# Head 0's query and key projections moved into the last attention group of a hybrid decoder step

## The chip, the cores and the metric

The kernel runs on one core of a Trainium2 chip. The metric is device time in microseconds (us) of one execution. Before the change the median of 3 runs is 2359.29 us (2358.37 to 2360.00); one more execution was profiled.

## The reference, cut to what matters

One layer, one step, for a prompt of 1024 tokens and 8 single sample tokens (1032 columns together). The part around the change:

```
h = rms_norm(x); proj = h @ w_in     # [dilated attention q/k/v of 3 groups | DeltaNet q/k/v | z | beta | decay | gates]
# branch A: per group (window, dilation) = (128,1), (512,4), (2048,16): 4 heads of 64, softmax with a relative bias,
#           groups merged by their softmax denominators; the sample tokens attend to cached keys and values
# branch B: per head (8 heads of 128): causal conv of width 4 + SiLU on q/k/v, l2norm, gated delta rule in chunks,
#           gated RMSNorm with silu(z)
x = x + rms_norm((sigmoid(gate_a) * (o_a @ w_a) + sigmoid(gate_b) * (o_b @ w_b)) @ w_out)
x = x + rms_norm((silu(h2 @ w_gate) * (h2 @ w_up)) @ w_ffn_out)      # h2 = rms_norm(x)
```

All is float32. A projection is computed in three passes: weights and inputs are split into a high and a low part, and lo*hi, hi*lo and hi*hi are added in one bank.

## The kernel before, in words

The program is written engine by engine: each engine has its instructions in a fixed order, and semaphores join them. A block of the program ends on all engines before the next begins.

**Attention block** (`attention_block`, L490). It normalises the input, then runs the three groups. A group has a key/value projection, a query projection (`q_part`), and 8 tiles of 128 queries (`tile`). While the tiles of a group run, TensorE fills its waits with the key/value projection of the next group (a `Filler`: a list of numbered steps, worked off up to a given number at given places). The last group (`AHEAD`, g = 2) has no next one, so its filler is empty. A tile is: scores on TensorE (L655), scale and bias, maximum and its negative on VectorE (L827, L832, L835), exponentials on ScalarE (L731), transposes on TensorE (L689), copy by ScalarE (L769), products with the values (L699), copy to `os_` by VectorE (L794), and a store of `os_` from SP's queue (L610). `os_` has two buffers: the maximum of tile t waits for the store of tile t - 2. In the last group the scores are issued two tiles ahead.

**Heads block** (`heads_block`, L2260). Head 0 has a stage of its own (the prologues near the end of the block), later heads are projected while the head before is in its recurrence. A head's projection has tiles m = 2, 3, 4, 5 (q, k, v, z), each of three thirds of 344 columns, each third 8 steps of three matmuls (L293 to L295): step numbers run from 49 to 144. On TensorE a third of tile m waits until the same third of tile m - 1 is read out of its bank (`evac`). ScalarE splits the weights' high part (`hi`, L286), reads the thirds out (L2435, L2437) and does the tanh of each convolution (L2448); VectorE splits the low part (`lo`, L289), does the convolution (L2523 to L2531) and the SiLU (L2501). ScalarE's order per tile, which stays as it is:

```python
if m < end:
    yield n + 2 * KT
    read_out(m, 1)
if before in CONVS:
    yield n + 2 * KT + 2
    tanh_of(CONVS.index(before))
if m < end:
    yield n + 3 * KT
    read_out(m, 2)
```

so the tanh of the tile before stands ahead of the last third's read-out. Between these steps stands the sample tokens' attention over cached keys: query rows (`queries`), spread of the queries over partitions on TensorE (L2063, L2064), scores against the cached keys on VectorE (L2132, L2136), softmax, turned probabilities (L2078), and last the products with the cached values (L2096). The constants for the convolutions (L1962 to L1975) and the weights that merge the groups (L2210 to L2229) stand there as well. Which step numbers come before which of these parts is written in `SPREAD_STEP`, `SC_STEP`, `P_STEP` (L2361). After the products VectorE takes the result (L2181) and clears `ub`, and head 0's recurrence begins.

Of the kernel before, what the change touches and what calls it, by code (L numbers as in the profile page):

```python
# [21 lines left out]
NS = 8  # L22
# [56 lines left out]
def build(nc, a, o):  # L79

    ctx = ExitStack()
    with ctx:
        n_names = [0]

        def sb(stack, name, shape, dt=FP):
            return stack.enter_context(nc.sbuf_tensor(name, shape, dt))

# [402 lines left out]
        def attention_block(used):  # L490

            with ExitStack() as s:
                KV, Q = 2 * HA * HD, HA * HD
                kv_hi = sb(s, "a_kv_hi", [P, KT, KV], FR); q_hi = sb(s, "a_q_hi", [P, KT, Q], FR)

                with ExitStack() as place:
                    kv_raw = sb(place, "a_kv_raw", [P, KT, KV]); q_raw = sb(place, "a_q_raw", [P, KT, Q])
                kv_lo = sb(s, "a_kv_lo", [P, KT, KV], FR); q_lo = sb(s, "a_q_lo", [P, KT, Q], FR)
# [48 lines left out]
                def wt(eng, name, g, k):  # L547
                    if E[name].at(g, k) > 0:
                        eng.wait_ge(E[name].sem, E[name].at(g, k))

# [21 lines left out]
                def _(sp):  # L572
# [11 lines left out]
                    for g in range(NG):  # L584
# [33 lines left out]
                def _(pe):  # L618
# [60 lines left out]
                    def tile(g, t, fill):  # L679
# [12 lines left out]
                        if g == AHEAD and t + 2 < NT:  # L692
                            scores(g, t + 2)
# [9 lines left out]
                        inc(last, "pv")  # L703

# [3 lines left out]

                    beta_pe(pe)
# [3 lines left out]
                def _(act):  # L713
# [45 lines left out]
                    def tile(g, t, fill):  # L759
# [11 lines left out]
                        if g == AHEAD and t + 1 < NT:  # L771
                            exps(g, t + 1)
# [15 lines left out]
                def _(v):  # L788
# [29 lines left out]
                    def tile(g, t, fill):  # L818
# [34 lines left out]
                    groups(v, kv_steps, beta_rest, q_part, tile, 1)  # L853

# [1086 lines left out]
        norm_sems = []  # L1941
        attention_block(norm_sems)
# [50 lines left out]
        def sample_attention(s, v_c, k_c, vec, ten, exped):  # L1993
# [18 lines left out]
            k_ld = [sem("sa_k") for _ in range(NG)]; v_ld = sem("sa_v")  # L2012
# [4 lines left out]
            def load(sp, stage):  # L2017
# [4 lines left out]
                if stage == 0:  # L2022
# [4 lines left out]
                    for g in range(NG):  # L2027
                        sp.dma_start(k_c[g][:NKEY[g]], rows(g, 0)).then_inc(k_ld[g], 16)
# [229 lines left out]
        pre = [sb(hs, f"pre{m}", [P, 3 + T]) for m in range(3)]  # L2258

        def heads_block(used):  # L2260
            s = hs
            w_raw = [sb(s, f"w_raw{j}", [P, KT, P]) for j in range(2)]
            w_hi = [sb(s, f"w_hi{j}", [P, KT, P], FR) for j in range(2)]
            w_lo = [sb(s, f"w_lo{j}", [P, KT, P], FR) for j in range(2)]
# [5 lines left out]
            with ExitStack() as place:  # L2270
# [5 lines left out]
                k_c = [sb(place, f"sa_k{j}", [P, NS, HA * HD]) for j in range(NG)]  # L2276
# [4 lines left out]
            k_tok = sb(s, "k_tok", F8); vb = sb(s, "vb", F8); kbe = sb(s, "kbe", F8); kdec = sb(s, "kdec", F8)  # L2281
# [3 lines left out]
            w_t = sb(s, "w_t", F8); q_dec = sb(s, "q_dec", F8)  # L2285
# [19 lines left out]
            wld = [sem("w_loaded") for j in range(2)]  # L2305
            whi = [ev("w_hi", 3, 1) for j in range(2)]
            wlo = [ev("w_lo", 3, 1) for j in range(2)]
            tile_done = [ev("tile_done", 3, 1) for j in range(2)]
            group = [ev("group", 6, 2) for g in range(2)]
            evac = [ev("evac", 6, 2) for g in range(3)]  # L2310
# [9 lines left out]
                      samp_m=1, cn=3, s_sq=1, s_nm=1, s_ln=1, s_r=1, s_v=4, s_k=1, s_vn=1, s_bc=2, s_o2=1, s_rms=1,  # L2320
                      s_oln=2, s_ob=1, s_add=2, s_dec=1)
            E = {k: ev(k, n, -1 if k in ("ob", "ssq", "s_oln", "s_add") else 0) for k, n in D1.items()}
# [34 lines left out]

            def is_last(h):
                return isinstance(h, int) and h == HB
# [863 lines left out]
```

## Time and profile before

| | us |
|---|---|
| median of 3 runs | 2359.29 |
| profiled execution | 2358.57 |
| its span | 2356.8 |
| TensorE busy | 2238.1 (95%) |
| VectorE busy | 1241.2 (53%) |
| ScalarE busy | 729.2 (31%) |

The span goes from the first to the last instruction; 1.8 us of the execution lie outside it. A timeline row gives start, duration, engine, line, output and inputs, and in brackets how long the engine was idle before and what released it. A window row gives for a stretch its length, and the busy time with the number of instructions of TensorE, its weight loads, VectorE, ScalarE and GpSimd, then TensorE's granted clock as a share of 2.4 GHz (so 0.50 is 1.2 GHz), the DMA share and GB/s. A group row ends with busy us, mean ns of one, and the idle time before.

### The profile page before, as it was taken

The numbers are of one execution on the slowest core, as the hardware profiler recorded it, in microseconds if no ns is written. First come the engines' busy times: TensorE is split into PE (matmuls) and PEld (weight loads), VectorE is DVE, ScalarE is ACT, GpSimd is POOL, SyncE is SP. The second block draws the span as 40 slices with busy tenths as digits, with TensorE's granted clock in tenths as the row PEclk, the third lists the DMA queues.
The fourth block names the chain that finished last, engine by engine and source line by source line (L and its number), as shares of the span: only waits on it lengthen the run. The fifth ranks groups of instructions, "written<-read, shape, count | busy, mean of one in ns | idle before, by whom it ended". The sixth has DMA issues, their size and how long they took to land. (4 is left out here: it accounts for less than half of the span.)

```text
span 2356.8 us, 36214 instructions
## 1 busy us (share of the span) xinstructions
PE 2238.1 (95%) x14552; PEld 2085.2 (88%) x14552; DVE 1241.2 (53%) x2379; ACT 729.2 (31%) x1646; POOL 65.0 (3%) x76
## 2 busy tenths in 40 slices
PE   7999997999999999999999699997999999989998
PEld 4688986899999999999998699767999999968777
DVE  5123222746666676766666634446666666641233
ACT  5133323222433233242423301444323233231222
POOL 0000000010101001010101000000000000000000
PEclk9999997879999999999999899998999999999999
DMA  5020210711213121121212335422222222351332
GB/s 182 1 73 17 86 57 28 167 36 46 82 28 91 45 75 60 50 71 48 82 55 86 100 126 180 145 87 55 80 74 73 77 80 80 115 175 38 117 91 84
DMA packets 214916, 191.14 MB, mean 81 GB/s; under 512 B 33699, under 2 KB 187076, under 8 KB 214758
## 3 DMA queue, kind: packets, MB, share of 16 engines
q1 hardware_dynamic: 201660, 146.00, 21.5%
q10 hardware_dynamic: 10190, 32.95, 3.5%
q0 software_dynamic: 2944, 10.49, 1.7%
q8 instruction: 85, 1.39, 0.3%
q14 instruction: 37, 0.30, 0.0%
HBM read 137.96 MB, written 51.64 MB: 80 GB/s over the span
## 5 line engine op out<-in xcount | busy, mean ns | idle before, releaser
L293 PE MATMUL bank<-xT_hi,w_lo 128*128 128x344 f32 x1152 | 395.9, 344 | 4.9 <-DVE w_lo L289 4.9
L294 PE MATMUL bank<-xT_lo,w_hi 128*128 128x344 f32 x1152 | 370.1, 321 | 0.0
L295 PE MATMUL bank<-xT_hi,w_hi 128*128 128x344 f32 x1152 | 370.0, 321 | 0.0
L293 PEld LDWEIGHTS bank<-xT_hi,w_lo 128*128 128x128 f32 x1152 | 219.4, 190 | 6.0 <-DVE w_lo L289 5.4
L294 PEld LDWEIGHTS bank<-xT_lo,w_hi 128*128 128x128 f32 x1152 | 219.5, 191 | 0.0
L295 PEld LDWEIGHTS bank<-xT_hi,w_hi 128*128 128x128 f32 x1152 | 218.2, 189 | 0.0
L1141 PE MATMUL bank<-xT_lo,f_hi 128*128 128x258 f32 x704 | 199.0, 283 | 0.0
L1139 PE MATMUL bank<-xT_hi,f_lo 128*128 128x258 f32 x704 | 198.9, 282 | 0.0
L1143 PE MATMUL bank<-xT_hi,f_hi 128*128 128x258 f32 x704 | 198.7, 282 | 0.0
L1139 PE MATMUL bank<-f_thi,f_lo 128*128 128x258 f32 x528 | 149.4, 283 | 1.0 <-DVE f_tlo L1120 1.0
L1143 PE MATMUL bank<-f_thi,f_hi 128*128 128x258 f32 x528 | 149.3, 283 | 0.0
L1141 PE MATMUL bank<-f_tlo,f_hi 128*128 128x258 f32 x528 | 148.9, 282 | 0.0
L1143 PEld LDWEIGHTS bank<-xT_hi,f_hi 128*128 128x128 f32 x704 | 133.1, 189 | 0.0
L1141 PEld LDWEIGHTS bank<-xT_lo,f_hi 128*128 128x128 f32 x704 | 132.9, 189 | 0.0
L1139 PEld LDWEIGHTS bank<-xT_hi,f_lo 128*128 128x128 f32 x704 | 132.8, 189 | 0.0
L1139 PEld LDWEIGHTS bank<-f_thi,f_lo 128*128 128x128 f32 x528 | 99.8, 189 | 1.2 <-issue 1.2
L1141 PEld LDWEIGHTS bank<-f_tlo,f_hi 128*128 128x128 f32 x528 | 99.8, 189 | 0.0
L1143 PEld LDWEIGHTS bank<-f_thi,f_hi 128*128 128x128 f32 x528 | 99.5, 188 | 0.0
L2435 ACT ACTIVATE pre<-bank 128x344 f32<-128x344 f32 x72 | 32.0, 456 | 215.2 <-PE bank L295 159.5
L293 PE MATMUL bank<-a_kv_hi,xT_lo 128*128 128x512 f32 (+1 forms) x216 | 95.1, 440 | 0.0
L2531 DVE SCALAR_TENSOR_TENSOR qkv<-pre,conv_wt,qkv 128x1024 f32<-128x1024 f32 x72 | 92.1, 1279 | 0.0
L294 PE MATMUL bank<-a_kv_lo,xT_hi 128*128 128x512 f32 (+1 forms) x216 | 86.3, 400 | 0.0
(438 smaller groups left out, 5074.2 us busy)
## 6 DMA issues: line engine op xcount, KB each, us to landing
w_raw<-in_w_in SPq DMA_DIRECT2D x48, 512.0 KB, 3.9
f_raw<-in_w_ffn_in SPq DMA_DIRECT2D x44, 512.0 KB, 4.9
act_scr<-f_y ACTq DMA_DIRECT2D x22, 516.0 KB, 2.6
o_sr<-act_scr SPq DMA_DIRECT2D x16, 704.0 KB, 6.5
o_wr<-in_w_ffn_out SPq DMA_DIRECT2D x22, 512.0 KB, 5.7
gate_scr<-gate ACTq DMA_DIRECT2D x16, 516.0 KB, 3.3
mix_ta<-gate_scr SPq DMA_DIRECT2D x8, 516.0 KB, 4.9
mix_tb<-gate_scr SPq DMA_DIRECT2D x8, 516.0 KB, 5.8
```

What stands on the lines that cost most here:

```text
L293: nc.tensor.matmul(out, stat_lo, mov_hi, start=start, stop=False)
L294: nc.tensor.matmul(out, stat_hi, mov_lo, start=False, stop=False)
L295: return nc.tensor.matmul(out, stat_hi, mov_hi, start=False, stop=stop)
L1139: nc.tensor.matmul(bank, lo[j][:, a, k], x_hi[:, k], start=opens and k == 0, stop=False, skip_group_check=True)
L1141: nc.tensor.matmul(bank, hi[j][:, a, k], x_lo[:, k], start=False, stop=False, skip_group_check=True)
L1143: last = nc.tensor.matmul(bank, hi[j][:, a, k], x_hi[:, k], start=False, stop=k == 3, skip_group_check=True)
L2435: x = nc.scalar.activation(pre[CONVS.index(x)][:, 3 + g * G3:3 + (g + 1) * G3], src, ACT.Copy)
L2531: nc.vector.scalar_tensor_tensor(y[:, :L], x_[:, tap:tap + L], cw[:, tap:tap + 1], y[:, :L], ALU.mult, ALU.add).then_inc(conv.sem, 1)
```

## The change

The query and key projections of head 0 (tiles m = 2 and 3, 48 steps) are issued within the tiles of the last attention group: three steps after a tile's transposes and scores, four after its products, in tiles 1 to 7, in the banks 7 and 3 that this group leaves free. Their weights, those of the value projection and the cached keys of the first two groups are loaded into the memory of the attention weights once the last query projection is done, from SP's queue, ahead of the group's stores (the value weights ahead of tile 3's store). ScalarE reads the thirds out in the tiles and splits the weights, VectorE splits the low parts. The memory lies on the right side, where the attention weights now stand too. In the heads block the projection of head 0 starts at step 97, the loads at its start have another order (constants, statistics and merged rows, then the sample's inputs with the third group's keys, then z's weights), and the step numbers between which the parts stand are new, one set for each engine.

```diff
-        def attention_block(used):
+        def attention_block(used, begun, hd, hd_keys):
...
-                kv_hi = sb(s, "a_kv_hi", [P, KT, KV], FR); q_hi = sb(s, "a_q_hi", [P, KT, Q], FR)
-
-                with ExitStack() as place:
-                    kv_raw = sb(place, "a_kv_raw", [P, KT, KV]); q_raw = sb(place, "a_q_raw", [P, KT, Q])
-                kv_lo = sb(s, "a_kv_lo", [P, KT, KV], FR); q_lo = sb(s, "a_q_lo", [P, KT, Q], FR)
+                with ExitStack() as weights:
+                    kv_hi = right(weights, "a_kv_hi", [P, KT, KV], FR); q_hi = right(weights, "a_q_hi", [P, KT, Q], FR)
+                    with ExitStack() as place:
+                        kv_raw = right(place, "a_kv_raw", [P, KT, KV]); q_raw = right(place, "a_q_raw", [P, KT, Q])
+                    kv_lo = right(weights, "a_kv_lo", [P, KT, KV], FR); q_lo = right(weights, "a_q_lo", [P, KT, Q], FR)
+                    right(weights, "a_rest", [P, 32])
+                w_raw = [right(hd, f"w_raw{j}", [P, KT, P]) for j in range(2)]
+                w_hi = [right(hd, f"w_hi{j}", [P, KT, P], FR) for j in range(2)]
+                w_lo = [right(hd, f"w_lo{j}", [P, KT, P], FR) for j in range(2)]
+                pre = [right(hd, f"pre{m}", [P, 3 + T]) for m in range(2)]
+                k_c = [right(hd_keys, f"sa_k{j}", [P, NS, HA * HD]) for j in range(2)]
+                wld = [sem("w_loaded") for j in range(2)]
+                whi = [ev("w_hi", 3, 1) for j in range(2)]
...
+                PER_TILE = 7
+                early_bank = (7, 3)
+
+                def steps_by(t):
+                    return PER_TILE * t if t < NT - 1 else 6 * KT
+
+                def at_tile(n):
+                    m, g = 2 + n // 3, n % 3
+                    return m, g, m % 2, m // 2
+
+                def head_load(sp, m):
+                    j, u = m % 2, m // 2
+                    if u > 1:
+                        sp.wait_ge(wlo[j].sem, wlo[j].at(0, u))
+                    c = HEAD_COLUMNS[m - 2]
+                    sp.dma_start(w_raw[j][:], w_in[:, :, c:c + P]).then_inc(wld[j], 16)
+
+                def head_hi(act, m):
+                    j, u = m % 2, m // 2
+                    if u > 1:
+                        act.wait_ge(tile_done[j].sem, tile_done[j].at(0, u))
+                    act.wait_ge(wld[j], u * 16)
+                    split_weights_hi(act, w_hi[j][:], w_raw[j][:]).then_inc(whi[j].sem, 1)
+
+                def head_lo(v, m):
+                    j, u = m % 2, m // 2
+                    v.wait_ge(whi[j].sem, whi[j].at(0, u + 1))
+                    split_lo(v, w_lo[j][:], w_raw[j][:], w_hi[j][:]).then_inc(wlo[j].sem, 1)
+
+                def head_steps(pe):
+                    for n in range(6):
+                        m, g, j, u = at_tile(n)
+                        for k in range(KT):
+                            yield n * KT + k + 1
+                            if k == 0 and g == 0:
+                                pe.wait_ge(wlo[j].sem, wlo[j].at(0, u + 1))
+                            if k == 0 and n >= 2:
+                                m2, g2, _, _ = at_tile(n - 2)
+                                pe.wait_ge(evac[g2].sem, evac[g2].at(0, m2 + 1))
+                            c = slice(g * G3, (g + 1) * G3)
+                            last = passes(banks[early_bank[n % 2]][:, :G3], w_hi[j][:, k], w_lo[j][:, k],
+                                          xT_hi[:, k, c], xT_lo[:, k, c], k == 0, k == KT - 1)
+                        last.then_inc(group[g].sem if g < 2 else tile_done[j].sem, 1)
+
+                def head_read_out(act, n):
+                    m, g, j, u = at_tile(n)
+                    if g < 2:
+                        act.wait_ge(group[g].sem, group[g].at(0, m + 1))
+                    else:
+                        act.wait_ge(tile_done[j].sem, tile_done[j].at(0, u + 1))
+                    nc.scalar.activation(pre[m - 2][:, 3 + g * G3:3 + (g + 1) * G3], banks[early_bank[n % 2]][:, :G3],
+                                         ACT.Copy).then_inc(evac[g].sem, 1)
...
+                        if g == AHEAD:
+                            wt(sp, "kvd", g, 9)
+                            wt(sp, "qd", g, 6)
+                            for m in (2, 3):
+                                head_load(sp, m)
+                            for n, (name, every) in enumerate((("cache_kv_w128", 1), ("cache_kv_w512", 4))):
+                                sp.dma_start(k_c[n][:], a[name][0].rearrange("b r s h d -> r b s (h d)")[::every, :, 0]
+                                             ).then_inc(k_ld[n], 16)
                         for t in range(NT):
+                            if g == AHEAD and t == 3:
+                                head_load(sp, 4)
...
-                        if g == AHEAD and t + 2 < NT:
-                            scores(g, t + 2)
+                        if g == AHEAD:
+                            if t + 2 < NT:
+                                scores(g, t + 2)
+                            if t:
+                                head.upto(steps_by(t - 1) + 3)
...
+                        if g == AHEAD:
+                            head.upto(steps_by(t))
...
-                        if g == AHEAD and t + 1 < NT:
-                            exps(g, t + 1)
+                        if g == AHEAD:
+                            for n in range(6):
+                                if t and steps_by(t - 2) < (n + 1) * KT <= steps_by(t - 1):
+                                    head_read_out(act, n)
+                            if t + 1 < NT:
+                                exps(g, t + 1)
+                            if t < 2:
+                                head_hi(act, 2 + t)
+                        if g == AHEAD and t == NT - 1:
+                            head_hi(act, 4)
+                            head_read_out(act, 5)
+                            for m in range(2):
+                                act.wait_ge(evac[2].sem, evac[2].at(0, m + 3))
+                                nc.scalar.activation(conv_new[:, m * HB:m * HB + 1], pre[m][:, L:L + 3 + NS].unsqueeze(1),
+                                                     ACT.Copy).then_inc(cn.sem, 1)
...
+                        if g == AHEAD and t in (1, 2):
+                            head_lo(v, 1 + t)
                         if t == NT - 1:
                             out_copy(g, t)
+                            if g == AHEAD:
+                                head_lo(v, 4)
...
-                    for g in range(NG):
-                        sp.dma_start(k_c[g][:NKEY[g]], rows(g, 0)).then_inc(k_ld[g], 16)
+                    sp.dma_start(k_c[2][:NKEY[2]], rows(2, 0)).then_inc(k_ld[2], 16)
...
+            def begun_before(h, m):
+                return h == 0 and m < FIRST
...
 
-            SPREAD_STEP, SC_STEP, P_STEP = (64, 82, 98), 112, 130
+            FIRST = 4
+            PE_SPREAD, PE_SC, PE_P = (0, 104, 116), 128, 136
+            V_SPREAD, V_SC, A_SC = (0, 0, 90), 94, 113
...
+                    if begun_before(h, m):
+                        continue
...
-                            if first is not None and first != (m < 4):
+                            if prev is None and m <= FIRST:
...
-                    load(0, None, first=True)
                     constants_load(sp)
+                    merge_load(sp)
                     sa_load(sp, 0)
-                    merge_load(sp)
-                    load(0, None, first=False)
+                    load(0, None)
...
-                            fill.upto(SPREAD_STEP[g])
+                            fill.upto(PE_SPREAD[g])
-                        fill.upto(SC_STEP)
+                        fill.upto(PE_SC)
-                        fill.upto(P_STEP)
+                        fill.upto(PE_P)
-                        fill.upto(SC_STEP)
+                        fill.upto(A_SC)
-                            fill.upto(SPREAD_STEP[g])
+                            fill.upto(V_SPREAD[g])
-                        fill.upto(SC_STEP - 3)
+                        fill.upto(V_SC)
```

## Rows read from the trace of the kernel before

**Rows 1.** Windows by stage (columns as above: engines, clock, DMA share, GB/s)

```profile
366.50:407.20 40.70, 29.55 (x162) 24.60 (x160) 15.96 (x48) 18.40 (x74) 0.00 (x0) 0.72 0.07 24
409.30:424.30 15.00, 8.31 (x49) 6.61 (x49) 3.79 (x11) 3.40 (x3) 0.00 (x0) 0.61 1.02 243
424.30:479.50 55.20, 55.20 (x333) 53.24 (x332) 44.59 (x90) 12.12 (x23) 0.00 (x0) 0.93 0.56 132
479.50:502.70 23.20, 23.20 (x109) 22.53 (x108) 2.31 (x2) 2.69 (x3) 0.00 (x0) 0.59 0.00 1
```

**Rows 2.** Windows of TensorE alone: last group's query projection; first query spread

```profile
345.00:365.00 20.00, 20.00 (x129) 1.00 0.35 130
432.27:434.35 2.08, 2.08 (x18) 1.00 0.86 140
```

**Rows 3.** Timeline of TensorE, last attention group (start, us, engine, line, tile)

```profile
395.16 1.22 PE L655 MATMUL bank<-a_kT,a_qT 64*128 64x128 f32 x8
396.31 1.16 PE L699 MATMUL bank<-a_kv,a_pT 128*128 128x128 f32 x8
399.60 0.66 PE L689 MATMUL bank<-ident,a_sc 128*128 128x128 f32 x4 [2.13 <-ACT a_sc L731]
```

**Rows 4.** Timeline of VectorE, last attention group, tiles 0 and 2

```profile
376.37 0.49 DVE L794 COPY a_os<-bank 128x128 f32<-128x128 f32 x2 [4.56 <-PE bank L699]
...
378.72 0.69 DVE L832 TENSOR_REDUCE a_os<-a_sc 128x4 f32<-128x512 f32 x1 [1.20 <-DMA att_scr<-a_os]
```

**Rows 5.** Timeline of SP's queue, start of head 0's stage

```profile
412.66 0.48 SPq L1957 DMA_DIRECT2D norm_dv<-in_norm_delta  x1
```

**Rows 6.** Timeline of TensorE, head 0's stage

```profile
420.94 1.90 PE L1962 MATMUL bank<-ident,sa_v 28*128 28x28 f32 x24 [1.71 <-DMA norm_dv<-in_norm_delta]
...
490.97 11.75 PE L2096 MATMUL bank<-sa_pT,sa_v 128*128 128x2 f32 x48
```

**Rows 7.** Timeline of VectorE, head 0's stage

```profile
421.64 0.17 DVE L2107 COPY sa_by_row<-ident 8x32 f32<-8x32 f32 x1 [5.98 <-DMA sa_onehot<-in_c_onehot_s]
...
425.88 0.94 DVE L2123 TENSOR_REDUCE sa_self<-sa_own 8x12 f32<-8x768 f32 x1
...
433.55 0.19 DVE L2210 TENSOR_TENSOR m_top<-m_stats 128x32 f32<-128x32 f32 x1 [4.59 <-DMA m_stats<-att_scr]
...
436.34 2.47 DVE L2132 TENSOR_TENSOR sa_k<-sa_k,bank 128x512 f32<-128x512 f32 x4
...
465.67 0.15 DVE L2143 COPY sa_of_row<-bank 32x8 f32<-32x8 f32 x1
...
472.59 0.38 DVE L2168 COPY sa_pT<-bank 128x32 f32<-128x32 f32 x3 [2.28 <-PE bank L2078]
...
475.46 0.74 DVE L2523 TENSOR_SCALAR qkv<-pre,conv_wt 128x1032 f32<-128x1032 f32 x1
...
481.71 1.23 DVE L2501 SCALAR_TENSOR_TENSOR qkv<-tanh,qkv 128x1032 f32<-128x1032 f32 x1 [1.13 <-ACT tanh L2448]
```

**Rows 8.** Groups of VectorE, 409 to 505 us (busy us, mean ns, idle before)

```profile
L2132 DVE TENSOR_TENSOR sa_k<-sa_k,bank 128x512 f32<-128x512 f32 (+1 forms) x12 | 7.4, 676 | 0.0
L2136 DVE TENSOR_REDUCE sa_sc<-sa_k 128x32 f32<-128x2048 f32 (+1 forms) x3 | 6.8, 2283 | 0.1
L289 DVE TENSOR_TENSOR w_lo<-w_raw,w_hi 128x1024 fp32r<-128x1024 f32 x5 | 6.1, 1215 | 8.0 <-ACT w_hi L286 8.0
...
L1973 DVE COPY conv_state<-bank 128x288 f32<-128x288 f32 x2 | 0.9, 437 | 0.0
```

**Rows 9.** Groups of ScalarE, 409 to 505 us

```profile
L286 ACT ACTIVATE w_hi<-w_raw 128x1024 fp32r<-128x1024 f32 x5 | 5.3, 1054 | 4.1 <-DMA w_raw<-in_w_in 4.1
L2435 ACT ACTIVATE pre<-bank 128x344 f32<-128x344 f32 x9 | 4.0, 452 | 20.2 <-PE bank L295 20.2
```

**Rows 10.** Windows with weight loads (411), third keys (426) in transfer

```profile
411.00:414.00 3.00, 0.00 (x0) 0.00 (x0) 0.00 (x0) 0.65 (x1) 0.00 (x0) 0.50 1.12 308
...
426.00:429.00 3.00, 3.00 (x12) 3.00 (x11) 2.96 (x10) 0.00 (x0) 0.00 (x0) 0.50 1.08 137
```

More of the change, by code:

```diff
@@ L707, in beta_rest @@
                         beta_over(pe)
+                    head = Filler(head_steps(pe))
                     beta_pe(pe)
@@ L2011, in sample_attention @@
             st = sb(s, "sa_st", [R, 4]); pT = sb(s, "sa_pT", [P, NG, R])
-            k_ld = [sem("sa_k") for _ in range(NG)]; v_ld = sem("sa_v")
+            k_ld.append(sem("sa_k")); v_ld = sem("sa_v")
             const_ld, moved = sem("sa_const"), sem("sa_moved")
@@ L2275, in heads_block @@
                     v_c[:CS, :2].rearrange("p g b c -> p (g b c)")[:, :3 * D])
-                k_c = [sb(place, f"sa_k{j}", [P, NS, HA * HD]) for j in range(NG)]
+                k_c.append(sb(place, "sa_k2", [P, NS, HA * HD]))
                 (sa_load, sa_turn_q, sa_bias, sa_spread, sa_turn_sc, sa_turn_p, sa_products, sa_exps, sa_q, sa_scores, sa_softmax,
@@ L2448, in tanh_of @@
                     nc.scalar.activation(tanh[:], qkv[n][:], ACT.Tanh).then_inc(thalf.sem, 1)
-                if first:
-                    yield 0
-                    hi(h, first)
-                yield 1
-                hi(h, first + 1)
+                if h:
+                    if first:
+                        yield 0
+                        hi(h, first)
+                    yield 1
+                    hi(h, first + 1)
+                else:
+                    yield 1
+                    hi(h, FIRST + 1)
                 for m in range(first, end + 1):
                     n, x, before = m * STEPS, kind.get(m, "end"), kind.get(m - 1, "none")
-                    if m < end:
+                    fresh = not begun_before(h, m)
+                    if m < end and fresh:
                         yield n + KT
@@ L2462, in project_act @@
                         gate_out(GATES.index(before))
-                    if m < end:
+                    if m < end and fresh:
                         yield n + 2 * KT
@@ L2468, in project_act @@
                         tanh_of(CONVS.index(before))
-                    if m < end:
+                    if m < end and fresh:
                         yield n + 3 * KT
                         read_out(m, 2)
-                    if m + 2 < end:
+                    if m + 2 < end and (h or m + 2 > FIRST + 1):
                         yield n + 3 * KT
@@ L2477, in project_act @@
                         hi(h + 1, 0)
-                    if x in CONVS:
+                    if x in CONVS and fresh:
                         c = CONVS.index(x)
@@ L2502, in silu_of @@
                                                    ALU.mult).then_inc(silu.sem, 1)
-                if first:
-                    yield 0
-                    lo(h, first)
-                yield 1
-                lo(h, first + 1)
+                if h:
+                    if first:
+                        yield 0
+                        lo(h, first)
+                    yield 1
+                    lo(h, first + 1)
+                else:
+                    yield 1
+                    lo(h, FIRST + 1)
                 for m in range(first, end + 1):
@@ L2535, in project_dve @@
                         silu_of(cm)
-                    if m + 2 < end:
+                    if m + 2 < end and (h or m + 2 > FIRST + 1):
                         yield n + 3 * KT
@@ L3093, in _ @@
                     pipelined(v, project_dve, recur_dve, 1, prologue)
-        att_sems = list(live)
+        att_sems = [x for x in live if all(x is not y for y in begun)]
         heads_block(att_sems)
@@ L3100, in build @@
         hs.close()
+        hd.close()
         mix_stack = ExitStack()
```

40 lines of the change are left out of this document (21 added, 19 removed).

## Prediction, made before the changed kernel was built or run

> **What bounds the kernel now.** I read the stage table first, because the chain of waits at the end of the page covers the last stage only and says nothing of the place changed. Two stages matter. In the last attention group (366.5 to 407.2 us) TensorE is busy for 29.55 of 40.70 us, and the granted clock is 0.72, so much of it ran at 1.2 instead of 2.4 GHz [rows 1]. Here the chain per tile ends: exponentials, transposes, copy, products, store, and TensorE waits in it. Then head 0's stage starts at 409.3. Its first 15 us are loads (TensorE 8.31 busy, clock 0.61), from 424.3 to 479.5 TensorE is busy without a gap while VectorE has 44.59 us of work in the same 55.20, and from 479.5 to 502.7 TensorE alone does the cached values' small products at clock 0.59 [rows 1]. So TensorE ends the stage today, but VectorE is not far behind it. The reader is to see both: an idle engine in one stage, and a second engine right under the first in the other.
>
> **What the change moves.** 48 steps of three 344-column matmuls leave head 0's stage and stand between the tiles of the last group: three steps ahead of a tile's products, four behind, in tiles 1 to 7. Six read-outs, three splits on ScalarE and three on VectorE go with them, and 1.5 MB of weights and 2 MB of keys are loaded from SP's queue before the stores of the group. Behind it, the order of head 0's stage is new on all engines.
>
> **The last group, step by step.** At full clock such matmuls start every 20.00/129 = 0.155 us, 0.157 without the edges [rows 2], so a step is 0.47 us and the 48 are 22.6. A tile's own work at that clock is 0.6 for transposes (399.60), 1.15 for scores (395.16 to 396.31) and 1.1 for products [rows 3]. Tile 0 stays as it is. In tile 1 the steps wait for the first low half of the weights: VectorE copies tile 0 out until 376.86 [rows 4], the split takes 1.2 [rows 8], so 378.1. Three steps, products and four steps end at 378.1 + 1.4 + 1.1 + 1.9 = 382.5. TensorE then never waits: tiles 2 to 5 take 0.6 + 1.15 + 1.1 + 7 x 0.47 = 6.15 each (24.6), tile 6, which has no scores to issue, 5.0, and tile 7 up to its products 3.1: 415.2, and 415.8 with the copy-out, against 407.2 now [rows 1]. The other loop, over the store, does not decide: from products to the second next transposes it needs copy-out (0.5), store (1.9 from 376.86 to 378.72) and reduction (0.7) [rows 4], and some 2.3 for exponentials and hand-offs, 5.4 in all, and TensorE now brings some 8 us of its own work between. ScalarE's read-outs (0.45 each) and splits (1.05) [rows 9] fall into its gaps. Behind the last products ScalarE has the last three steps (1.4), a read-out and two small copies, about 2.3 us; the store that it stands beside takes as long. So this stage is **8.7 us longer**. Bounds: it can't be under 3 (TensorE's work alone, 29.55 at clock 0.72, is 21.3 at full clock; with 22.6 that is 43.9 against 40.7 [rows 1]); with a tile or two at the low clock, or a late store, 13.
>
> **Head 0's stage, step by step, from its own start.** What leaves TensorE is 22.6 us and more at the low clock; but what then ends the stage is VectorE's order. Offsets in us:
> Today VectorE's first inputs are there at 421.64 - 409.34 = 12.3 [rows 7]. The two weights (1 MB at 308 GB/s, 3.4) go out from ahead of them, the merged rows (1 MB, between 2.9 and 3.4) and three loads of statistics come in ahead (0 to 3.8, 1.5 taken): **13.3** [rows 10].
> The query rows take 421.64 to 426.8, 5.2: 18.5. Then VectorE stands before the low half of z's weights, which load last, behind the third group's keys: 512 KB of keys at 137 GB/s (3.8) and 512 KB at 308 (1.7) [rows 10] land at 18.8; split high 1.05, low 1.2 [rows 8, 9]: 21.2. This is a new wait, and behind it in VectorE's queue are the constants, which the first query spread on TensorE waits for. Constants 1.1 (two copies of 0.44 and small ones) [rows 8], merge weights 433.55 to 436.34, 2.8 [rows 7]: 25.1. The spread, at 22.4, takes 2.08 at full clock [rows 2] and at most double at half; TensorE was idle for some ten us, so 3.5: 25.9.
> Scores of group 0 are (7.4 + 6.8)/3 = 4.75 [rows 8]: 30.7. Meanwhile TensorE does the first third of the value projection, 24 matmuls, 3.8 at full and 7.5 at half clock, 5.3 taken: 31.2; second spread 33.3; scores of group 1: 38.1. Query convolution 475.46 to 480.58, 5.1 [rows 7]: 43.2. Scores of group 2: 48.0; SiLU 1.2: 49.2. Softmax to the diagonal, 465.67 to 470.31: 53.8. Turning the probabilities on a waiting TensorE 0.7 and the copies 0.7 [rows 7]: 55.2.
> Now the key convolution, which stands behind the probabilities: 60.3. ScalarE's tanh of it, 1.1 [rows 7], 61.4, is queued ahead of the read-out of the value projection's last third (0.45, 61.9), and TensorE can't start the last third of z before that bank is read. So it stands idle from about 54.5 to 62. The third (24 matmuls, 3.8 to 7.5, 5.5 taken after such a pause) ends at 67.5, and the products take the 23.2 that they take now [rows 1]: 90.7, and 91.4 with some seven hand-offs of 0.1. Today the last product ends at 490.97 + 11.75 - 409.34 = 93.4 [rows 6]. What VectorE still has to do (value convolution, splits) is hidden under the products. The stage is **2 us shorter**, with bounds from 12 shorter (z's last third not waiting, loads early) to 4 longer (all of the two thirds and the products at the low clock).
>
> **Clock.** The rows show that the stretch with waits ran at 0.61 and the gapless one at 0.93 [rows 1]. The Trainium skill (TensorE: Matmul & The Clock Gate, HAM oscillation — how this bites in real kernels) says that an engine that waits for data between bursts runs each burst at the lower clock; the trace agrees, and by the rule the group gains and head 0's stage, now with more pauses, loses. Both are in the values taken above.
>
> **Sum.** 8.7 - 2 = +6.7 on the profiled execution's 2358.57 us, of which 1.8 lie outside its span: 2365.3. The median of the runs is 0.7 higher: **2366**. Everything behind head 0's stage is as before.
>
> **Rivals.**
> *TensorE stays the bound of head 0's stage (faster).* Then the steps' time goes out of it whole, 22.6 / 0.93 = 24, and the two weights' load from its start (3.4): 8.7 - 27.7 = -19, 2340. For it: TensorE is gapless there today. It decides at one point: VectorE's probabilities and key convolution must be done before TensorE reaches z's last third. Against it: 44.59 us of VectorE's work within those 55.20 us [rows 1], of which only two splits go. Half of it (z's last third not held, keys and constants early by 2 us) gives 8.7 - 15 or 2353. 0.19.
> *The two ends cancel (no change).* z's last third waits, but loads land 2 to 3 us earlier and the clock holds: heads 6 to 8 us shorter, about 2359. 0.23.
> *The stores stand behind the loads (slower still).* A 0.5 KB load issued at 412.66 kept TensorE waiting until 420.94, behind 1.7 MB [rows 5, 6]: the queue is worked off in order. Tile 0's store comes at 376.9, and 3 MB in front of it, from 366.5 at 308 GB/s and a start of 1 us, take until 377.7: some 1 us, hidden by the steps. At 137 GB/s it would be 389, tile 2 would start 9 us later and at half clock: 2374. The Trainium skill (DMA: Bandwidth & Descriptors, Queues, rings and completion order) says that each engine takes its descriptors in ring order, which those rows bear out; by its rule alone the store can only be late, and how much is the rate's matter. 0.10.
> That the projections don't fit between the tiles at all is excluded: their banks and weights are there by tile 1.
>
> **How the numbers follow.** The forecast has 0.48; its own range is 2361 to 2371. Under 0.2% (4.7 us) a run can't be told from no change. Faster is the first rival with the edge of the second, 0.20; same is most of the second, and the forecast's lower edge where the group's +8.7 meets a stage 5 us shorter, 0.24; slower 0.56. The range reaches from 2353, the half form of the first rival, to 2374, the third.
>
> **What would show it.** In the last group: tiles of 6.2 us at clock 1.0, no wait of the reduction for a store beyond 1 us, the heads stage starting near 418. In head 0's stage: VectorE before z's low half at about 18 to 20; TensorE idle for 5 to 8 us ahead of z's last 24 matmuls, released by ScalarE's read-out; products starting 65 to 70 us after the stage's start (70.2 now). I'm wrong if the products start under 60, or if tiles take under 5.5.

## The result and the profile after

The changed kernel takes 2363.95 us in the median of 20 runs (2361.63 to 2371.60), the kernel before 2359.61 in 20 runs beside them (2355.44 to 2364.19): ratio 1.0023, 95% interval 1.0016 to 1.0030, 4 to 7 us slower. In a later set on one chip the ratio was 1.0035 (1.0021 to 1.0049). The forecast was 2366.

The profiled execution of after took 2367.45 us, 8.88 more than that of before. Cut at marks that both traces have: 1.6 arise ahead of the last group's first copy-out (378.00 against 376.37), in a part whose instructions no edit touches and that varied between 376.2 and 382.3 over the profiles of this study. From that copy-out to the first load of head 0's stage it is 40.44 us against 32.97: **+7.5**. The stage from there to the clearing of the result rows is 96.2 against 94.4: **+1.8**. The rest is 2.0 shorter; in the other profiles it varies over 3 us, and what sets it stays open.

The same two stretches in before, then the stages of after, as in [rows 1] (stretch, its length, busy time and instructions of TensorE, its weight loads, VectorE, ScalarE and GpSimd, granted clock, DMA share, GB/s): the group from its first copy-out, the loads, the scores and convolutions, the products.

```profile
376.37:409.34 32.97, 22.79 (x124) 18.75 (x122) 12.82 (x40) 13.95 (x55) 0.00 (x0) 0.71 0.10 34
409.34:503.73 94.39, 86.73 (x489) 82.37 (x489) 51.35 (x105) 18.21 (x29) 0.00 (x0) 0.79 0.49 116
```
```profile
378.00:418.44 40.44, 39.12 (x268) 37.13 (x266) 16.52 (x43) 18.37 (x65) 0.00 (x0) 0.98 0.17 53
418.44:443.02 24.58, 5.19 (x37) 4.05 (x37) 7.19 (x22) 2.34 (x2) 0.00 (x0) 0.55 0.66 122
443.02:489.57 46.55, 37.57 (x200) 35.24 (x200) 38.80 (x76) 7.18 (x13) 0.00 (x0) 0.80 0.36 91
489.57:513.68 24.11, 24.08 (x109) 23.43 (x108) 1.71 (x2) 2.69 (x3) 0.00 (x0) 0.56 0.00 1
```

The group is now TensorE's without a gap at full clock. Head 0's stage has changed bound: TensorE, gapless before once the loads were in ([rows 1], from 424.3 on), is idle for 19 of the first 24.6 us and for 9 of the next 46.6, at a lower clock. What it waits for there (sum, times, longest):

```profile
PE bank L296 <- ACT pre L2542: 8.5, 2, 6.9
PE bank L2159 <- DVE sa_trep L2218: 7.8, 1, 7.8
PE bank L2072 <- DMA norm_dv<-in_norm_delta: 6.3, 1, 6.3
PE bank L2172 <- DVE conv_wt L2085: 5.3, 1, 5.3
```

L2542 is ScalarE's read-out of a projection third, and its 6.9 us stand ahead of z's last third. VectorE's and ScalarE's timelines show both chains (start, duration, line, operation; in brackets the idle time before and its releaser). First VectorE, beside [rows 7]:

```profile
435.67 0.17 DVE L2216 COPY sa_by_row<-ident 8x32 f32<-8x32 f32 x1 [18.32 <-DMA sa_onehot<-in_c_onehot_s]
440.78 1.20 DVE L292 TENSOR_TENSOR w_lo<-w_raw,w_hi 128x1024 fp32r<-128x1024 f32 x1
443.02 0.19 DVE L2319 TENSOR_TENSOR m_top<-m_stats 128x32 f32<-128x32 f32 x1
446.93 2.48 DVE L2241 TENSOR_TENSOR sa_k<-sa_k,bank 128x512 f32<-128x512 f32 x4 [1.05 <-PE bank L2173]
455.01 2.48 DVE L2241 TENSOR_TENSOR sa_k<-sa_k,bank 128x512 f32<-128x512 f32 x4 [3.28 <-PE bank L2173]
475.94 0.38 DVE L2281 COPY sa_pd<-bank 8x32 f32<-8x32 f32 x3
```

The small constants (the sample's table and one-hot rows, which VectorE waits for first) come 17.2 us after the stage's start at 418.44 (12.3 before). Then ScalarE and TensorE around z's last third:

```profile
438.97 1.06 ACT L289 ACTIVATE w_hi<-w_raw 128x1024 fp32r<-128x1024 f32 x1 [19.25 <-DMA w_raw<-in_w_in]
481.39 1.06 ACT L2555 ACTIVATE tanh<-qkv 128x1032 f32<-128x1032 f32 x1 [6.97 <-DVE qkv L2647]
482.36 0.44 ACT L2542 ACTIVATE pre<-bank 128x344 f32<-128x344 f32 x1
```
```profile
482.85 0.66 PE L296 MATMUL bank<-xT_hi,w_lo 128*128 128x344 f32 x1 [6.95 <-ACT pre L2542]
483.30 0.49 PE L297 MATMUL bank<-xT_lo,w_hi 128*128 128x344 f32 x1
```

The probabilities are copied at 476.3, but in TensorE's order z's last third stands in front of the products, and it waits for a read-out that stands behind the tanh of the key's convolution. After the wait its matmuls start every 0.29 us instead of the 0.157 of [rows 2].

### The profile page after: what moved, and what is told of

Same layout as the page of the kernel before. It is cut to its first block and busy times, and to the rows that moved or that the text cites. A ratio compares the mean times of both kernels' runs of the same rounds, so it can differ in the third digit from the quotient of the medians.

```text
span 2365.7 us, 36215 instructions
## 1 busy us (share of the span) xinstructions
PE 2233.5 (94%) x14552; PEld 2082.5 (88%) x14552; DVE 1243.0 (53%) x2379; ACT 728.5 (31%) x1646; POOL 64.6 (3%) x76
## 5 line engine op out<-in xcount | busy, mean ns | idle before, releaser
L296 PE MATMUL bank<-a_kv_hi,xT_lo 128*128 128x512 f32 (+1 forms) x216 | 95.2, 441 | 0.0
L2542 ACT ACTIVATE pre<-bank 128x344 f32<-128x344 f32 x66 | 29.3, 456 | 194.9 <-PE bank L298 139.2
```

The lines of the kernel that those rows point to most:

```text
L296: nc.tensor.matmul(out, stat_lo, mov_hi, start=start, stop=False)
L2542: x = nc.scalar.activation(pre[CONVS.index(x)][:, 3 + g * G3:3 + (g + 1) * G3], src, ACT.Copy)
```

## The experiments

All edits are to the changed kernel. "Group" is the time from the last group's first copy-out to the stage's first load, "stage" from that load to the clearing of the result rows; by these marks a profile can be read without the variation ahead of them. The unedited kernel has 40.4 and 96.0 to 96.2.

**e1_readout**: v's last third is read out ahead of the exponentials and the key's tanh.

```diff
+if h == 0 and m == FIRST:
+    yield n + 2 * KT
+    read_out(m, 2)
 if before in CONVS:
     yield n + 2 * KT + 2
     tanh_of(CONVS.index(before))
-if m < end and fresh:
+if m < end and fresh and (h or m > FIRST):
     yield n + 3 * KT
     read_out(m, 2)
```

> One edit to the changed kernel: for head 0, ScalarE reads the value projection's last third out right behind its second third, ahead of the exponentials and of the key's tanh. Theory (VectorE's key convolution, through the tanh queued ahead of that read-out, holds z's last third): the idle time of TensorE ahead of z's last 24 matmuls (8.5 us in the trace of the changed kernel) nearly goes, z's last third starts near 476 instead of 482.8 us, the products end 5 to 7 us earlier, median near 2358. Rival (VectorE's order decides anyway, or the clock takes it back): the products wait for something else, and the time stays within 1.5 us of the changed kernel's 2364.

Measured: 2355.98 us, ratio to before 0.9991 (0.9982 to 1.0000), 7.5 us under the changed kernel by the first set's ratio, 10 by the later one's. The 6.9 us ahead of z's last third are gone (the 1.6 us that are left for L2542 stand ahead of z's first third, as before the edit), and the products start 60.6 us after the stage's start instead of 71.1; the stage is 85.9, 10.3 shorter, more than the theory's 5 to 7. TensorE's waits in it:

```profile
PE bank L2159 <- DVE sa_trep L2218: 7.4, 1, 7.4
PE bank L2072 <- DMA norm_dv<-in_norm_delta: 5.9, 1, 5.9
PE bank L2172 <- DVE conv_wt L2085: 5.3, 1, 5.3
PE bank L296 <- ACT pre L2542: 1.6, 1, 1.6
```

The read-out's place in ScalarE's queue is shown to be the cause of that wait. The gain is larger than the wait because of the clock: without the pause z's last third takes 4.0 us instead of 6.7.

```profile
479.26 0.43 PE L296 MATMUL bank<-xT_hi,w_lo 128*128 128x344 f32 x1
483.24 0.84 PE L2199 MATMUL bank<-sa_pd,sa_own 8*128 8x16 f32 x6
```

**e2_smallfirst**: the small loads ahead of the merge's.

```diff
 constants_load(sp)
-merge_load(sp)
 sa_load(sp, 0)
 load(0, None)
+merge_load(sp)
```

> One edit to the changed kernel: in head 0's stage SP issues the own rows, table, one-hot rows, third group's keys and z's weights ahead of the merge's three statistics loads and its rows. Theory (the statistics, 32 KB each, are worked off slowly and hold the small constants behind them): VectorE's first wait of the stage ends near 12.5 us after its start instead of 17.2, all of VectorE's chain comes 4 to 5 us earlier, median 2359 to 2360. Rival (the statistics then come late and VectorE's wait only moves from the constants to the merge's weights): m_top waits 4 to 5 us, median near 2364.

Measured: 2359.77 us, ratio 1.0007 (0.9998 to 1.0016). VectorE's first wait ends 9.1 us after the stage's start, z's low half and the merge weights do not wait, and the stage is 89.9, 6.3 shorter. The wait ends 3.4 us before the theory's 12.5; the median is in its range, and the rival's wait for the statistics is not there:

```profile
426.41 0.17 DVE L2216 COPY sa_by_row<-ident 8x32 f32<-8x32 f32 x1 [10.22 <-DMA sa_onehot<-in_c_onehot_s]
433.97 0.19 DVE L2319 TENSOR_TENSOR m_top<-m_stats 128x32 f32<-128x32 f32 x1
```

**e3_fewsteps**: only 6 of the 48 steps stand in the group; the kernel leaves the other 42 out.

```diff
+if k < KT - 1:
+    continue
 c = slice(g * G3, (g + 1) * G3)
 last = passes(banks[early_bank[n % 2]][:, :G3], w_hi[j][:, k], w_lo[j][:, k],
-              xT_hi[:, k, c], xT_lo[:, k, c], k == 0, k == KT - 1)
+              xT_hi[:, k, c], xT_lo[:, k, c], True, True)
```

> The changed kernel with only the last of each eight steps of the query and key projections issued in the last attention group (6 of 48 steps; 126 of 144 matmuls are left out, so queries and keys of head 0 are incomplete); loads, splits and read-outs stay. It prices the steps where they stand. Theory (the group is 7.5 us longer because TensorE is gapless with them): the group falls back to near 41 us, 6 to 8 us less, median 2356 to 2358. Rival (steps fill idle time only; what lengthens the group is the loads, splits and read-outs): the group stays within 2 us, median near 2363.

Measured: 2358.02 us, ratio 1.0004 (0.9995 to 1.0013). The group is 32.93 (before 32.97), with all loads, splits and read-outs still in it:

```profile
376.51:409.44 32.93, 23.36 (x142) 19.21 (x140) 16.41 (x43) 18.27 (x65) 0.00 (x0) 0.87 0.21 64
```

So the steps alone make the 7.5 us. The stage behind it is 97.4, no shorter than with the steps.

**e4_value_early**: the value projection in the time of the loads.

```diff
 sa_turn_q(pe)
-fill.upto(52)
+fill.upto(120)
 constants_turn(pe)
```

> One edit to the changed kernel: TensorE runs the whole value projection of head 0 (24 steps) at the start of head 0's stage, while the loads come, instead of a third behind each query spread. Theory (the first third stands ahead of the second spread, at 1.2 GHz, and VectorE waits 3.3 us for it): that wait goes, the scores of the second group start 3 us earlier, median 2360 to 2361, if the key's convolution then passes it on; z's last third still waits about 8 us. Rival (z's last third waits for VectorE's key convolution whatever TensorE did before, and VectorE's chain is set by something else): within 1.5 us of 2364.

Measured: 2363.65 us, ratio 1.0025 (1.0016 to 1.0034): no gain that is told from none, as the rival has it. In its profile z's last third waits 6.9 us as before. The stage is 92.3, 3.7 shorter than in the second profile of the unedited kernel (next). VectorE's wait at the second spread is 1.62 us instead of 3.55, which is what the theory named; and the small constants landed at 13.4 instead of 15.6. In this execution the merge's megabyte, behind which they stand, landed 6.2 us after its issue; in the five other profiles with the same loads ahead it took 7.6 to 9.6. Why is open.

**after_again**: the changed kernel, unedited.

> The changed kernel once more, unedited, beside the others of this set. In its first profile VectorE's wait for the small constants ended 17.2 us into head 0's stage, and in four kernels with the same loads in the same order or nearly so between 13.4 and 16.5. Theory (the time at which they land varies by some us from execution to execution, and the profile taken first was a late one): this wait ends between 13 and 16.5, and the stage from its first load to the clearing of the result rows is 92 to 95 us instead of 96.2. Rival (17 is the rule): 17 again and 96. The last group from its first copy-out to that load: 40.4 us by both. Median 2363 to 2364.

Measured: 2366.47 us, group 40.4. The small constants end VectorE's wait at 15.6, in the theory's range, but the stage is 96.0, the rival's: the 1.7 us won at them are lost again where VectorE waits for TensorE, at the second spread (3.55 us instead of 3.28) and the turned scores (1.45 instead of 0.18). The stage is 96 in both profiles.

**e12**: e1 and e2 together.

> The changed kernel with both edits at once: ScalarE reads the value projection's last third out ahead of the exponentials and of the key's tanh, and SP issues the small constants, the third group's keys and z's weights ahead of the merge's statistics. Theory (two separate terms of one chain: VectorE's chain up to the probabilities, and behind it TensorE's wait for the read-out): the gains add, 7 for the one and 3 to 5 for the other, median 2351 to 2354. Rival (with one gone TensorE's own order decides, so that the second brings nothing): 2356, as the first edit alone.

Measured: 2349.23 us, ratio 0.9967 (0.9955 to 0.9979). The stage is 78.8: 17.2 to 17.4 shorter, where e1 and e2 alone have 10.3 and 6.3. The terms add, as the theory has it; the median is 2 us below its range.

**stats_last**: only the three statistics loads go behind z's weights.

```diff
-merge_load(sp)
+merge_load(sp, 0)
 sa_load(sp, 0)
 load(0, None)
+merge_load(sp, 1)
```

Part 0 is the megabyte of rows, part 1 the statistics (the function's own lines are not shown).

> The changed kernel with only the merge's three statistics loads (3 x 32 KB) moved behind z's weights; the merge's rows (1 MB) stay ahead of the small constants. Theory (it is the statistics, in very small pieces, that hold the constants, not the megabyte): VectorE's first wait of the stage ends 11 to 12.5 us after its start instead of 15.5 to 17.2, stage 91 to 93 us, median near 2360. Rival (the megabyte holds them): 14 us or more, and hardly a gain.

Measured: 2363.99 us, ratio 1.0018 (1.0008 to 1.0028), so the gain in time is not told from none. The small constants land at 12.8 and the stage is 93.8, both just outside the theory's ranges:

```profile
429.81 0.17 DVE L2216 COPY sa_by_row<-ident 8x32 f32<-8x32 f32 x1 [13.89 <-DMA sa_onehot<-in_c_onehot_s]
```

With 9.1 in e2 the megabyte costs 3.7 us, and the statistics 2.6 to 4.4 on top, for a tenth of the bytes, against five profiles with both ahead (15.4 to 17.2). The split rests on one execution of stats_last, and the early execution of e4, at 13.4, is only 0.6 behind it. What does not vary as much is SP's time to issue the three: 3.7 to 4.6 us in all six profiles, e4's among them. So both hold the small constants, and the statistics' share is known to a few us only.

**keys_late**: the cached keys of groups 0 and 1 go back into head 0's stage.

```diff
-for n, (name, every) in enumerate((("cache_kv_w128", 1), ("cache_kv_w512", 4))):
-    sp.dma_start(k_c[n][:], ...).then_inc(k_ld[n], 16)
...
-sp.dma_start(k_c[2][:NKEY[2]], rows(2, 0)).then_inc(k_ld[2], 16)
+for g in range(NG):
+    sp.dma_start(k_c[g][:NKEY[g]], rows(g, 0)).then_inc(k_ld[g], 16)
```

> One part of the change undone: the cached keys of groups 0 and 1 (2 MB) are loaded in head 0's stage again, ahead of the third group's keys and z's weights; the rest as changed. Theory (SP's queue is worked off in order, so z's weights land 6 to 8 us later, VectorE stands before their low half, and everything behind it in VectorE's queue waits): stage 100 to 103 us instead of 96, z's high half split 26 to 28 us after the stage's start instead of 19 to 20.5, median 2368 to 2372. Rival (the loads are hidden either way): stage 95 to 97, median 2363 to 2366. The last group 40.4 us by both, or 0.5 less if the keys stood ahead of its stores.

Measured: 2371.35 us, ratio 1.0052 (1.0039 to 1.0066). The group is 40.4 all the same, the stage 103.8, and the forecast's new wait is there:

```profile
446.19 1.23 DVE L292 TENSOR_TENSOR w_lo<-w_raw,w_hi 128x1024 fp32r<-128x1024 f32 x1 [7.72 <-ACT w_hi L289]
```

The keys' early load is worth nearly 8 us of the stage and costs the group nothing.

**best**: a new order of head 0's stage on all engines (small loads first; v while they come; VectorE's scores and softmax ahead of all convolutions; z before the probabilities).

```diff
-PE_SPREAD, PE_SC, PE_P = (0, 104, 116), 128, 136
-V_SPREAD, V_SC, A_SC = (0, 0, 90), 94, 113
+PE_SPREAD, PE_SC, PE_P = (120, 125, 130), 136, 144
+V_SPREAD, V_SC, A_SC = (1, 1, 1), 71, 120
...
+for m in range(FIRST, 5):
...
+    for g in range(3):
+        yield m * STEPS + (g + 1) * KT
+        read_out(m, g)
...
+yield 121
+tanh_of(0)
+tanh_of(1)
...
```

> Head 0's stage of the changed kernel in another order on all engines, its last attention group unchanged: the small loads first, TensorE does the whole value projection while they come and z's between the query spreads and before the probabilities, VectorE does scores and softmax ahead of all three convolutions, ScalarE the read-outs ahead of exponentials and tanh. Theory (VectorE's chain up to the probabilities sets the products' start, and the convolutions, some 20 us, fit under the products' 22): the products start 43 to 47 us after the stage's start instead of 71, the stage is 68 to 72 us instead of 96, median 2337 to 2342. Rival (TensorE's 48 steps of the value and z projections do not fit before the products at the clock granted, or the convolutions stick out behind them): products start at 52 or later, median 2347 or more.

Measured: 2341.33 us, ratio 0.9935 (0.9921 to 0.9948). The products start 45.9 us after the stage's start, and the stage is 70.2.

```profile
376.23:416.64 40.41, 39.09 (x268) 37.10 (x266) 16.53 (x43) 18.40 (x65) 0.00 (x0) 0.98 0.17 53
416.64:462.52 45.88, 42.89 (x237) 39.66 (x237) 28.20 (x74) 5.87 (x10) 0.00 (x0) 0.78 0.66 146
462.52:485.90 23.38, 23.34 (x108) 22.69 (x108) 19.60 (x26) 6.15 (x8) 0.00 (x0) 0.58 0.08 24
```

VectorE's 19.6 us in the last stretch are nearly all the three convolutions with their SiLU, now under the products.

**half**: the same order, with 24 of the 48 steps (the queries) in the group.

```diff
-PER_TILE = 7
+PER_TILE = 4
...
-FIRST = 4
+FIRST = 3
...
```

> As the kernel with head 0's stage in another order, but only the query projection (24 of the 48 steps, four a tile) stands within the last attention group; the key projection is done at the start of head 0's stage, in the time of the loads. Theory (each step in the group costs its time there once the idle time of 33 us is filled, while the stage's first 12 to 15 us on TensorE are idle anyway): the group from first copy-out to the stage's first load is 35 to 37 us instead of 40.4, the stage no longer than that of the other kernel, median 3 to 5 us below it. Rival (the steps filled the waits of the group and pulled its clock up, so half of them leave it as long as all; and 34 us of steps in the stage delay the products): no gain or 2 us slower.

Measured: 2337.95 us, ratio 0.9922 (0.9909 to 0.9936), the lowest median of all.

```profile
377.43:411.40 33.97, 29.00 (x196) 25.72 (x194) 16.52 (x43) 17.00 (x61) 0.00 (x0) 0.95 0.20 62
411.40:461.57 50.17, 49.61 (x310) 46.62 (x310) 28.25 (x74) 7.68 (x14) 0.00 (x0) 0.91 0.59 133
461.57:485.55 23.98, 23.94 (x108) 23.29 (x108) 19.59 (x26) 6.45 (x8) 0.00 (x0) 0.56 0.09 23
```

The first 24 steps, 11.3 us at full clock, make the group 1.0 us longer than before's 32.97, less than the theory's 2 to 4; the second 24 another 6.4. The 1.0 is not clear of the variation: with 6 steps or none the group took 32.9 to 35.2 us in four kernels (below). In the stage the key projection costs 4.9 us (75.1 against 70.2): much of it fits into the time of the loads, but the theory had the stage no longer.

**none** and **none2**: the same order with no step in the group; only the loads and splits of the query and key weights and the keys' loads are early.

```diff
-head.upto(steps_by(t - 1) + 3)
...
-head.upto(steps_by(t))
...
-FIRST = 4
+FIRST = 2
...
```

> As the kernel with head 0's stage in another order, but no step at all stands within the last attention group: only the query and key weights' loads, their splits and the cached keys' loads are there; both projections are done from the start of head 0's stage on. With 24 and 48 steps in the group it makes a curve: the group took 34.0 and 40.4 us, the stage 75.1 and 70.2. Theory (the first 24 steps filled time in which TensorE stood idle in the group, and in the stage TensorE is then the bound): group 33, stage 78 to 82 us, median 2341 to 2346, slower than with 24. Rival (moving the steps brings nothing, the order of head 0's stage does it all): stage 75 or less, median 2338 or less.

Measured: 2360.54 us, ratio 1.0011 (1.0001 to 1.0020), group 33.3, stage 96.6. Both missed the stage: it has two waits that I wrote into it (VectorE 8.4 us before z's low half, and TensorE 5.4 us for VectorE behind that). none2 takes them out:

```diff
-PE_SPREAD, PE_SC, PE_P = (80, 88, 96), 106, 144
-V_SPREAD, V_SC, A_SC = (1, 60, 60), 71, 120
+PE_SPREAD, PE_SC, PE_P = (80, 88, 96), 106, 120
+V_SPREAD, V_SC, A_SC = (1, 1, 1), 71, 112
...
-fill.upto(72)
+fill.upto(80)
```

> As the kernel without steps in the group, with two waits of its own order taken away: z's low half stands behind all three scores on VectorE (its high half waits for the key projection on TensorE), the exponentials ahead of the value's last read-out, and the probabilities are turned ahead of z's projection. Theory (without steps in the group TensorE is the bound of the stage: 96 steps of 0.47 us are 45 us, with some 10 us of small matmuls ahead of the products and 24.5 of products, against 33.2 in the group): stage 78 to 83 us, median 2342 to 2346, so 4 to 8 us slower than with 24 steps in the group and still faster than before. Rival (the move into the group is worth nothing, the order does it all): stage 75 or less, median 2338 or less.

Measured: 2352.42 us, ratio 0.9977 (0.9967 to 0.9986), slower than the theory's 2342 to 2346. The group is 35.2, the stage 86.6; from its start to the products TensorE is busy for 63.0 of 63.3 us.

```profile
411.95:475.29 63.34, 63.04 (x381) 60.21 (x381) 39.10 (x87) 11.04 (x20) 0.00 (x0) 0.89 0.52 114
```

So TensorE is the bound there as the theory says, but needs 63 us and not 55. By the ratios, 0.9977 and 0.9922, it is 13 us behind half. That is about what 24 steps in the group are worth in such a stage: 24 steps are 11.3 us at full clock. The two kernels differ in the order of the stage as well, so the 13 us are not the steps' alone.

none and none2 have the same instructions in the group, and it took 33.3 and 35.2 us, at a granted clock of 0.81 and 0.65:

```profile
377.36:410.61 33.25, 21.22 (x124) 17.26 (x122) 15.20 (x42) 15.02 (x56) 0.00 (x0) 0.81 0.14 47
376.71:411.95 35.24, 24.51 (x124) 20.12 (x122) 15.19 (x42) 15.01 (x56) 0.00 (x0) 0.65 0.13 44
```

## Why the prediction was right

The time came out as forecast, and the mechanism of both stretches is the forecast's. The stage moved the other way than forecast, though, and that the sum still lies so near is in part luck.

**The group: right, 1.2 us too long.** Forecast +8.7, measured +7.5. Tile 2's transposes came at 384.21, 6.21 us after the first copy-out; the forecast's 382.5 is 6.13 after 376.37. The tiles then took 5.98 us (transposes at 384.21, 390.19, 396.18), 6.15 forecast, with the group's granted clock at 0.98. e3 puts the whole length on the steps.

```profile
384.21 0.60 PE L771 MATMUL bank<-ident,a_sc 128*128 128x128 f32 x4
390.19 0.60 PE L771 MATMUL bank<-ident,a_sc 128*128 128x128 f32 x4
```

**The stage: its mechanism right, its sign wrong.** Forecast 2 shorter, measured 1.7 to 1.8 longer. The chain is the forecast's link by link: constants, scores, probabilities, key convolution, tanh, read-out, z's last third, products. TensorE's wait ahead of z's last third, forecast as some 7.5 us from 54.5 to 62, is 6.9 us and ends at 64.4, released by L2542; without it (e1) the stage is 10 us shorter. The mis-sized terms:

- *"three loads of statistics come in ahead (0 to 3.8, 1.5 taken)"*: by the one execution of stats_last they cost 2.6 to 4.4, and SP alone takes 3.7 to 4.6 to issue them. The megabyte cost 3.7 where 2.9 was taken. VectorE's wait ended at 15.6 and 17.2, not 13.3.
- *The new wait of VectorE before z's low half* (forecast from 18.5 to some 20, then the split to 21.2): the split of z's high half began at 20.5, where 18.8 was forecast, and VectorE, late itself, came to the low half at 22.3, later still. There was no such wait, and its 1.5 us come off the first error: 3.9 - 1.5 are the 2.4 us that z's last third is late in the first profile. keys_late shows that the mechanism is real: with 2 MB more in the queue it is 7.7 us.
- *z's last third* took 6.7 us instead of 5.5: all but its last few matmuls ran at the low clock after its pause, where "5.5 taken" was between the two. The products followed at 0.56.

Together: z's last third begins 2.4 us late and takes 1.2 more, the products 0.2 more: 95.2 to the last product instead of 91.4.

**The sum** came to +6.7 by two errors of opposite sign (-1.2 in the group, +3.8 in the stage are missing); by the profiles' marks it is +9.3. The medians, at +4.3 and +8.9 in two sets, do not part the two. The profiled execution of after is 3.5 us above the median of its set and that of before 1.0 below; where the first set's lower +4.3 comes from is open, as both profiles of the changed kernel have the same two stretches.

**The rivals.** *TensorE stays the bound* fell where it was said to decide: TensorE reached z's last third at 475.9, the probabilities were copied at 476.3, and the key convolution ended at 481.4. best and half turn that point round by another order and come near that rival's 2340, with 2341 and 2338. In best the stage is then 24 us shorter than before's, where the rival had 27.7. *The two ends cancel* fell: the small constants and z's weights landed later, not earlier. *Stores behind loads* fell: the reduction's longest wait for a store in the group is 1.7 us, and TensorE, gapless, does not feel it; without the keys in front (keys_late) the group is as long.

```profile
380.58 0.69 DVE L933 TENSOR_REDUCE a_os<-a_sc 128x4 f32<-128x512 f32 x1 [0.30 <-DMA att_scr<-a_os]
403.35 0.69 DVE L933 TENSOR_REDUCE a_os<-a_sc 128x4 f32<-128x512 f32 x1 [1.73 <-DMA att_scr<-a_os]
```

**The clock.** The Trainium skill (TensorE: Matmul & The Clock Gate, HAM oscillation — how this bites in real kernels) shows a kernel whose matmuls wait for data between bursts, so that each burst starts at the lower clock again. From it the forecast took that the group gains and head 0's stage loses. The traces agree: the group went from 0.71 to 0.98, and the stage's stretch with the convolutions, at 0.93 before [rows 1], runs at 0.80. Not every wait does it: after the 1.6 us ahead of z's first third the matmuls still start every 0.157 us, after the 6.9 us ahead of its last third every 0.29.

**The signs.** Of what the forecast said would show it, the start of the stage near 418 (418.4), the tiles at full clock and TensorE's idle time of 5 to 8 us ahead of z's last third (6.9, released by the read-out) came. Three others missed by a little: a reduction waited 1.7 us for a store instead of at most 1, VectorE came to z's low half at 22.3 instead of 18 to 20, and the products started at 71.1 instead of 65 to 70.

## What to carry to other kernels

Work moved into an engine's idle time is free only up to that idle time, and what fills it is read by adding steps: here 24 cost 1 us or less and the next 24 cost 6.4. When a bound is taken off one engine, go through the other engines' queues in order for the first entry that stands before something the freed engine needs; one read-out behind a tanh was worth 10 us, and one order of small loads 6. Only with these put right did the move pay: 2364 as changed, 2349 with the two, 2338 with a new order and half of the steps, against some 2358 before. What the new order would give the kernel before, with no load or step moved, was not run; the nearest is none2, at 2352.

## What was not expected

Three loads of 32 KB each took 4.2 us of SP's time to issue (420.63 to 424.85). By stats_last they delayed what stood behind them about as much as the 1 MB load did (2.6 to 4.4 against 3.7 us).

```profile
420.63 4.22 SPq L2308 DMA_DIRECT2D m_stats<-att_scr  x3
424.89 0.59 SPq L2310 DMA_DIRECT2D merged<-att_scr  x1
```

With 24 steps added, the group's granted clock rose to 0.95, from 0.71 in before and between 0.65 and 0.87 in none2, none and e3, which have no step or six in it. TensorE's busy time rose by 6.2 us (22.79 to 29.00) for steps that are 11.3 us at full clock: part of the work paid for itself by the clock.
